# Norms of input plus branch over alpha, the input carried as its two rounded halves

## The chip, the cores and the metric

The kernel runs on one core of a Trainium2 chip. Its time is device microseconds of that core. It is written in the Bass language: every engine (TensorE for matmuls, VectorE, ScalarE, GpSimd, and SyncE for transfers) has its own program, and semaphores order them. The kernel's time is the median of several runs; times of single instructions come from one profiled execution.

## The reference

Two layers of a first block (FFN, mixer of attention and mLSTM, FFN) are followed by two layers of a second block. The change is in the second block alone:

```python
DN_ALPHA = (2 * DEPTH) ** 0.25          # DEPTH = 2
LN_EPS = 1e-5

def second_block(x, ...):
    cos, sin = rotary_tables(x.shape[1])
    for l in range(DEPTH):
        y = hybrid_mixer(x, ..., cos, sin)             # ends in concat(ya, yb, yc, yd) @ w_o
        x = layer_norm(DN_ALPHA * x + y, ln1_g[l], ln1_b[l])
        y = conv_gated_ffn(x, ...)                     # ends in (silu(gate) * val) @ w_down
        x = layer_norm(DN_ALPHA * x + y, ln2_g[l], ln2_b[l])
    return x

def layer_norm(x, g, b):
    mu = mean(x);  var = mean((x - mu) ** 2)
    return (x - mu) * rsqrt(var + LN_EPS) * g + b
```

x has 256 tokens of 1024 features in fp32; the FFN width is 2816. A layer norm does not change when its input is divided by alpha, if its eps is divided by alpha squared.

## The kernel before

All weights come as units of 128x1024 fp32 through a ring: SyncE loads `w_raw`, ScalarE rounds it to `w_hi` (line 542), VectorE forms the remainder `w_lo` (line 1033), TensorE waits for both (`split_done`). Activations are kept as a rounded half and a remainder too (`h_hi`, `h_lo`; `ya_hi`, `ya_lo`; `act_hi`, `act_lo`), and every product is three matmuls on rounded operands: hi x hi, lo x hi, hi x lo (lines 1732 to 1734 with the weight tile loaded into the array and the activation streamed; lines 1738 to 1740 with the activation loaded and 512 columns of weights streamed). The order is written out by hand: each engine's program calls its steps unit by unit, and a step waits on a semaphore that another engine counts up.

In the second block, the residual x lives in `x_residual` with features on partitions, and `h_hi`, `h_lo` hold its rounded half and its remainder. The norms are taken with tokens on partitions: the last product of a stage (`w_o`, or `w_down`) adds up in the two accumulators `acc_tok`, 128 tokens x 1024 features each. The residual is brought into the same accumulator by TensorE, as a matmul with a scaled identity: `carry(t, k)` adds 128 features of token half t (line 2134). There are 16 carries per stage:

- `mixer2`: eight for t = 0 in a row behind unit 19 (`VALUES_AT`), eight for t = 1 in a row at the start of the second half of `tail_norm`.
- `conv_ffn`: one for t = 0 behind each of the first eight down units, eight for t = 1 in `tail_norm`.

`tail_norm` runs the last four units of a stage for t = 0, then the carries and the same four units for t = 1; meanwhile VectorE and ScalarE take the statistics of t = 0 and norm it (`layer_norm`, `y_tok`), TensorE turns the result back (`turn_norm`, line 2129), and it is rounded for the next stage.

The branch reaches the accumulator through these roundings, each a pair of ScalarE (hi) and VectorE (lo): `c_round` / `c_rest` (spatial gating), `d_round` / `d_rest` (pooling, with a per-feature scale), `o_round` / `o_rest` (attention, twice per mixer, unit 21), and in the FFN `act32`, the product of gate and value (line 1479), which `act_round` / `act_rest` split.

## Time and profile before

| what | value |
|---|---|
| median of 3 runs | 2004.33 us (2003.71 to 2005.48) |
| profiled execution | 2003.57 us, its span 2001.7 us |
| TensorE busy | 1983.4 us, 99% |
| TensorE weight loads | 1735.8 us, 87% |
| VectorE busy | 1265.5 us, 63% |
| ScalarE busy | 1100.1 us, 55% |
| mean granted TensorE clock | 0.998 |

The page names each group of instructions by its line, its engine, output<-inputs and shape. A tile name without number stands for all its buffers: `acc` is `acc_tok`, `stream` the four banks, `act` is `act32`. An fp32 matmul leaves two records and two weight loads, a matmul on rounded operands (fp32r) one of each. Matmul records overlap, so the time that one takes is read from the distance of starts or from the chain of waits, not from its duration.

### The profile page before, as it was taken

The page shows a single profiled execution, that of the slowest core. Times are in us where ns is not written, and L with a number is a line of the kernel's source. Part 1 is how long each engine was busy: PE and PEld are TensorE (multiplying, and loading weights), DVE is VectorE, ACT ScalarE, POOL GpSimd, SP SyncE. Part 2 cuts the span into 40 slices and gives each one's busy share as a digit, 9 for nine tenths or more (in the row PEclk, how much of TensorE's full clock was granted, in tenths as well). Part 3 has the DMA queues.
Part 4 walks back from the last instruction along what each step waited for, and adds up shares of the span by engine and source line. Part 5 has one row for each costly group of instructions (what it writes and reads, how often), then busy time and mean ns, then how long its engine had stood idle before and what let it go on. Part 6 is the DMA issues. An engine that isn't in the chain of part 4 may idle for free.

```text
span 2001.7 us, 29971 instructions
## 1 busy us (share of the span) xinstructions
PE 1983.4 (99%) x11884; PEld 1735.8 (87%) x11884; DVE 1265.5 (63%) x2121; ACT 1100.1 (55%) x1709; POOL 6.5 (0%) x17
## 2 busy tenths in 40 slices
PE   9999999999999999999999999999999999999998
PEld 7888898998888888889989988888899997889997
DVE  5555787566555655567846665557567776657775
ACT  5445676465544644466664564447455556545554
POOL 0000000000000000000000000000000000000000
PEclk9999999999999999999999999999999999999999
DMA  8665545555666466655464556664336665335662
GB/s 281 188 187 174 166 130 168 162 155 158 209 188 189 148 199 190 189 149 168 134 192 131 164 190 196 187 186 144 116 115 181 184 186 164 116 106 169 183 186 84
DMA packets 93690, 335.86 MB, mean 168 GB/s; under 512 B 10224, under 2 KB 12528, under 8 KB 93552
## 3 DMA queue, kind: packets, MB, share of 16 engines
q1 hardware_dynamic: 92112, 328.51, 53.7%
q0 software_dynamic: 720, 4.37, 0.5%
q8 instruction: 95, 1.56, 0.3%
q10 hardware_dynamic: 720, 1.07, 0.2%
q14 instruction: 43, 0.35, 0.1%
HBM read 332.86 MB, written 1.05 MB: 167 GB/s over the span
## 4 chain that ended last, share of the span: by engine, by line
PE 95%; DVE 3%; ACT 1%; issue 1%; DVEq 0%; ACTq 0%
PE stream L1732 11%; PE stream L1733 11%; PE stream L1734 10%; PE stream L1738 9%; PE stream L1740 9%; PE stream L1739 9%; PE acc L1738 8%; PE acc L1740 8%; PE acc L1739 8%; PE stream L1828 1%; PE acc L2279 1%; DVE w_lo L1033 1%; PE acc L2134 1%; PE stream L1791 1%; PE stream L1758 0%
## 5 line engine op out<-in xcount | busy, mean ns | idle before, releaser
L1033 DVE TENSOR_TENSOR w_lo<-w_raw,w_hi 128x1024 fp32r<-128x1024 f32 x624 | 760.8, 1223 | 407.9 <-ACT w_hi L542 407.0
L542 ACT ACTIVATE w_hi<-w_raw 128x1024 fp32r<-128x1024 f32 x624 | 655.5, 1055 | 420.1 <-PE stream L1740 207.9
L1732 PE MATMUL stream<-h_hi,w_hi 128*128 128x256 f32 (+1 forms) x1504 | 434.2, 289 | 2.5 <-DVE h_lo L1433 2.5
L1734 PE MATMUL stream<-h_hi,w_lo 128*128 128x256 f32 (+1 forms) x1504 | 424.7, 282 | 0.0
L1733 PE MATMUL stream<-h_lo,w_hi 128*128 128x256 f32 (+1 forms) x1504 | 424.6, 282 | 0.0
L1738 PE MATMUL stream<-w_hi,h_hi 128*128 128x512 f32 x864 | 342.1, 396 | 2.2 <-DVE h_lo L1433 2.2
L1740 PE MATMUL stream<-w_lo,h_hi 128*128 128x512 f32 x864 | 337.3, 390 | 0.0
L1739 PE MATMUL stream<-w_hi,h_lo 128*128 128x512 f32 x864 | 336.8, 390 | 0.0
L1732 PEld LDWEIGHTS stream<-h_hi,w_hi 128*128 128x128 f32 x1504 | 287.8, 191 | 10.5 <-issue 7.1
L1733 PEld LDWEIGHTS stream<-h_lo,w_hi 128*128 128x128 f32 x1504 | 288.0, 191 | 0.8
L1734 PEld LDWEIGHTS stream<-h_hi,w_lo 128*128 128x128 f32 x1504 | 287.6, 191 | 0.0
L1738 PE MATMUL acc<-w_hi,act_hi 128*128 128x512 f32 x528 | 211.2, 400 | 1.4 <-DVE act_lo L1105 1.3
L1740 PE MATMUL acc<-w_lo,act_hi 128*128 128x512 f32 x528 | 206.3, 391 | 0.0
L1739 PE MATMUL acc<-w_hi,act_lo 128*128 128x512 f32 x528 | 206.3, 391 | 0.0
L1738 PEld LDWEIGHTS stream<-w_hi,h_hi 128*128 128x128 f32 x864 | 162.5, 188 | 35.8 <-issue 2.5
L1740 PEld LDWEIGHTS stream<-w_lo,h_hi 128*128 128x128 f32 x864 | 162.4, 188 | 34.4
L1739 PEld LDWEIGHTS stream<-w_hi,h_lo 128*128 128x128 f32 x864 | 162.7, 188 | 31.8
L1467 DVE SCALAR_TENSOR_TENSOR conv_tiles<-stream,params,conv_tiles 128x255 f32<-128x255 f32 (+1 forms) x168 | 81.0, 482 | 66.0 <-ACT conv_tiles L870 63.0
L1738 PEld LDWEIGHTS acc<-w_hi,act_hi 128*128 128x128 f32 x528 | 99.4, 188 | 22.5 <-DVE w_lo L1033 3.0
L1740 PEld LDWEIGHTS acc<-w_lo,act_hi 128*128 128x128 f32 x528 | 99.1, 188 | 21.7
L1739 PEld LDWEIGHTS acc<-w_hi,act_lo 128*128 128x128 f32 x528 | 99.5, 188 | 17.8
L870 ACT ACTIVATE conv_tiles<-stream,params 128x256 f32<-128x256 f32 x84 | 47.5, 565 | 117.7 <-PE stream L1734 117.7
(308 smaller groups left out, 2291.4 us busy)
## 6 DMA issues: line engine op xcount, KB each, us to landing
w_raw<-in_w_up SPq DMA_DIRECT2D x264, 512.0 KB, 3.7
w_raw<-in_w_mix SPq DMA_DIRECT2D x228, 512.0 KB, 3.7
w_raw<-in_w_down SPq DMA_DIRECT2D x132, 512.0 KB, 3.7
params<-in_params POOLq DMA_DIRECT2D x4, 859.5 KB, 5.5
out_x<-x_residual SPq DMA_DIRECT2D x4, 256.0 KB, 2.4
constants<-in_consts POOLq DMA_DIRECT2D x1, 832.0 KB, 8.1
x_residual<-in_x ACTq DMA_DIRECT2D x3, 256.0 KB, 7.4
x_residual<-in_x SPq DMA_DIRECT2D x1, 256.0 KB, 3.5
```

What stands on the lines that cost most here:

```text
L542: nc.scalar.activation(w_hi[:, u % RING], w_raw[:, u % RAW], ACT.Copy).then_inc(hi_ready, 1)
L870: nc.scalar.activation(cbuf[:, 2 * (i % 2) + side_i], conv_tile(i, side_i), ACT.Identity, scale=p2("conv_w", (2 * 2 + side_i) * NF + i), b ...
L1033: nc.vector.tensor_tensor(w_lo[:, u % RING], w_raw[:, u % RAW], w_hi[:, u % RING].bitcast(F32), ALU.subtract).then_inc(split_done, 1)
L1467: r = nc.vector.scalar_tensor_tensor(out=cbuf[:, s, back:], in0=conv_tile(i, side_i)[:, 0:T - back], scalar=p2("conv_w", ((2 - back) * 2 + ...
L1732: nc.tensor.matmul(dst, w_hi[:, s, w], hi, start=first, stop=False)
L1733: nc.tensor.matmul(dst, w_hi[:, s, w], lo, start=False, stop=False)
L1734: return nc.tensor.matmul(dst, w_lo[:, s, w], hi, start=False, stop=last)
L1738: nc.tensor.matmul(dst, hi, w_hi[:, s, w], start=first, stop=False)
L1739: nc.tensor.matmul(dst, lo, w_hi[:, s, w], start=False, stop=False)
L1740: return nc.tensor.matmul(dst, hi, w_lo[:, s, w], start=False, stop=last)
L1791: r = nc.tensor.matmul(turned[1][:, t:t + 1], h32[:, k, half(t)], ones_model[:, 0:1], start=(k == 0), stop=(k == KT - 1))
L1828: r = nc.tensor.transpose(turned[c % 2][:, half(2 * i + t)], cbuf[:, 2 * (c % 2) + t, half(i)], ident)
```

## The change

The norms are taken of x + branch/alpha. The carry has no factor any more, so its operands can be the two halves that exist already, `h_hi` and `h_lo`, with the rounded identity `ident_rounded` of the first block's mixer. The factor 1/alpha moves into the roundings of the branch: into `c_round`, `o_round` (a scale), `c_rest`, `o_rest` and `act32` (scalar_tensor_tensor for tensor_tensor), and for the pooling into a small tile `pool_scale`, made once per layer. The norm's eps becomes `eps3`. The tile `ident_alpha` and TensorE's wait for it go.

```diff
@@ build
+        eps3, _ = sb("eps3", [P, 1])
-        ident_alpha, _ = sb("ident_alpha", [P, P])
+        pool_scale, _ = sb("pool_scale", [P, 2])
@@ ScalarE: layer_norm, mixer2, start
-                                         bias=eps2[:]).then_inc(act_step, 1)
+                                         bias=eps3[:]).then_inc(act_step, 1)
...
                 def c_round():
                     act.wait_ge(c_turned, l + 1)
-                    nc.scalar.activation(ya_hi[:, 4:6].rearrange("p a t -> p (a t)"), side[3][:],
-                                         ACT.Copy).then_inc(cd_hi, 1)
+                    nc.scalar.activation(ya_hi[:, 4:6].rearrange("p a t -> p (a t)"), side[3][:], ACT.Copy,
+                                         scale=1.0 / ALPHA).then_inc(cd_hi, 1)
                 def d_round():
                     act.wait_ge(d_mixed, l + 1)
+                    act.wait_ge(alpha_ready, l + 1)
                     for ct in range(2):
                         r = nc.scalar.activation(ya_hi[:, 6 + ct], bank[2][:, ct * T:(ct + 1) * T], ACT.Copy,
-                                                 scale=p2("pool_scale", ct))
+                                                 scale=pool_scale[:, ct:ct + 1])
...
-                                         ACT.Copy).then_inc(o2_hi, 1)
+                                         ACT.Copy, scale=1.0 / ALPHA).then_inc(o2_hi, 1)
...
-            act.wait_ge(init, 4)
+            act.wait_ge(init, 5)
@@ VectorE: conv_ffn, mixer2, start
-                    nc.vector.tensor_tensor(act32[:, i % 2], silu_g[:, i % 2], cbuf[:, 2 * (i % 2) + 1],
-                                            ALU.mult).then_inc(gated, 1)
+                    nc.vector.scalar_tensor_tensor(out=act32[:, i % 2], in0=silu_g[:, i % 2], scalar=1.0 / ALPHA,
+                                                   in1=cbuf[:, 2 * (i % 2) + 1], op0=ALU.mult,
+                                                   op1=ALU.mult).then_inc(gated, 1)
...
                 def o_rest(t):
                     dve.wait_ge(o2_hi, l * 2 + t + 1)
-                    nc.vector.tensor_tensor(ya_lo[:, 0:4, half(t)], bank[2 * t + 1][:].rearrange("p (k q) -> p k q", k=4),
-                                            ya_hi[:, 0:4, half(t)].bitcast(F32), ALU.subtract).then_inc(ab_split, 1)
-
-                if l == 0:
-                    nc.vector.tensor_scalar(ident_alpha[:], ident, ALPHA, None, ALU.mult).then_inc(alpha_ready, 1)
+                    nc.vector.scalar_tensor_tensor(out=ya_lo[:, 0:4, half(t)],
+                                                   in0=bank[2 * t + 1][:].rearrange("p (k q) -> p k q", k=4),
+                                                   scalar=1.0 / ALPHA, in1=ya_hi[:, 0:4, half(t)].bitcast(F32),
+                                                   op0=ALU.mult, op1=ALU.subtract).then_inc(ab_split, 1)
+
+                nc.vector.tensor_scalar(pool_scale[:], p2("pool_scale", 0, 2), 1.0 / ALPHA, None,
+                                        ALU.mult).then_inc(alpha_ready, 1)
...
+            nc.vector.memset(eps3[:], LN_EPS / ALPHA ** 2).then_inc(init, 1)
@@ TensorE: carry, mixer2
             def carry(t, k):
-                nc.tensor.matmul(acc_tok[t][:, k * P:(k + 1) * P], xr[:, k, half(t)], ident_alpha[:], start=False,
-                                 stop=False)
+                for x in (h_hi, h_lo):
+                    nc.tensor.matmul(acc_tok[t][:, k * P:(k + 1) * P], x[:, k, half(t)], ident_r[:], start=False,
+                                     stop=False)
...
-                        if i == V_OUT:
-                            pe.wait_ge(alpha_ready, 1)
```

`c_rest` changes as `o_rest` does, and `d_rest` reads `pool_scale` as `d_round` does.

The order of TensorE's instructions, at the first down unit of the first convolution FFN (`act_hi`, `act_lo` are the gated tile's halves), before:

```order
L1740 MATMUL acc<-w_lo,act_hi 128x512
L2134 MATMUL acc<-ident_alpha,x_residual 128x128
L1732 MATMUL stream<-h_hi,w_hi 128x256 [waits conv2_done,split_done]
L1733 MATMUL stream<-h_lo,w_hi 128x256
L1734 MATMUL stream<-h_hi,w_lo 128x256
```

and now:

```order
L1747 MATMUL acc<-w_lo,act_hi 128x512
L2142 MATMUL acc<-ident_rounded,h_hi 128x128
L2142 MATMUL acc<-ident_rounded,h_lo 128x128
L1739 MATMUL stream<-h_hi,w_hi 128x256 [waits conv2_done,split_done]
L1740 MATMUL stream<-h_lo,w_hi 128x256
L1741 MATMUL stream<-h_hi,w_lo 128x256
```

One fp32 instruction, which the trace shows as two passes, becomes two instructions on rounded operands; what stands around it keeps its place.

VectorE's order in the first mixer, from the attention's row scales to the tail's first statistics, before:

```order
L1609 RECIPROCAL row_scales<-row_sums 128x16 [waits e2_ready]
L1613 TENSOR_TENSOR o_tok<-stream,row_scales 128x512 [waits o2_ready,dve_step]
L1613 TENSOR_TENSOR o_tok<-stream,row_scales 128x512 [waits o2_ready]
L1033 TENSOR_TENSOR w_lo<-w_raw,w_hi 128x1024 [waits hi_ready] x2
L1620 TENSOR_TENSOR ya_lo<-stream,ya_hi 128x4x128 [waits o2_hi] x2
L1033 TENSOR_TENSOR w_lo<-w_raw,w_hi 128x1024 [waits hi_ready]
L1404 BN_STATS ln_stats<-acc 128x6 [waits acc_left]
```

and now:

```order
L1613 RECIPROCAL row_scales<-row_sums 128x16 [waits e2_ready]
L1617 TENSOR_TENSOR o_tok<-stream,row_scales 128x512 [waits o2_ready,dve_step]
L1617 TENSOR_TENSOR o_tok<-stream,row_scales 128x512 [waits o2_ready]
L1035 TENSOR_TENSOR w_lo<-w_raw,w_hi 128x1024 [waits hi_ready] x2
L1624 SCALAR_TENSOR_TENSOR ya_lo<-stream,ya_hi 128x4x128 [waits o2_hi] x2
L1035 TENSOR_TENSOR w_lo<-w_raw,w_hi 128x1024 [waits hi_ready]
L1406 BN_STATS ln_stats<-acc 128x6 [waits acc_left]
```

`o_rest` stands where it stood, in the other form; nothing else here moved.

## Rows read from the trace of the kernel before

**Rows 1.** Page: span, part 1, part 4 (chain that ended last) by engine.

```profile
span 2001.7 us, 29971 instructions
...
PE 1983.4 (99%) x11884; PEld 1735.8 (87%) x11884; DVE 1265.5 (63%) x2121; ACT 1100.1 (55%) x1709; POOL 6.5 (0%) x17
...
PE 95%; DVE 3%; ACT 1%; issue 1%; DVEq 0%; ACTq 0%
```

**Rows 2.** Waits of TensorE, two of seven: us in total, times, longest.

```profile
PE stream L2129 <- ACT y_tok L828: 3.9, 2, 3.3
...
PE acc L1738 <- DVE ya_lo L1620: 0.3, 2, 0.2
```

**Rows 3.** First convolution FFN: us, PE, PEld, DVE, ACT, POOL busy, clock, DMA.

```profile
1480.00:1672.00 192.00, 192.00 (x1384) 181.64 (x1384) 138.83 (x209) 107.49 (x161) 0.60 (x1) 1.00 0.60 180
```

**Rows 4.** Line 2134, the carries: count, ns min/median/max, first and last start.

```profile
L2134 PEld LDWEIGHTS acc<-ident_alpha,x_residual x128: 187/192/192, 1449.0 to 1985.7; 128*128 128x128 f32 x128
L2134 PE MATMUL acc<-ident_alpha,x_residual x128: 270/275/275, 1449.2 to 1985.8; 128*128 128x128 f32 x128
```

**Rows 5.** The chain that ended last, two of its pieces: start us, us, what.

```profile
1441.27 1.73 PE stream L2299 x16
...
1449.40 1.78 PE acc L2134 x16
```

**Rows 6.** TensorE's timeline behind a group of eight: start us, us, engine, line, what.

```profile
1450.94 0.48 PE L1738 MATMUL acc<-w_hi,ya_hi 128*128 128x512 f32 x1
1451.25 0.40 PE L1739 MATMUL acc<-w_hi,ya_lo 128*128 128x512 f32 x1
1451.49 0.39 PE L1740 MATMUL acc<-w_lo,ya_hi 128*128 128x512 f32 x1
```

**Rows 7.** TensorE's timeline, a lone carry in the convolution FFN.

```profile
1532.59 0.38 PE L2134 MATMUL acc<-ident_alpha,x_residual 128*128 128x128 f32 x2
...
1532.93 0.28 PE L1733 MATMUL stream<-h_lo,w_hi 128*128 128x256 f32 x1
1533.05 0.28 PE L1734 MATMUL stream<-h_hi,w_lo 128*128 128x256 f32 x1
```

**Rows 8.** TensorE's timeline, narrow rounded products, first and last of 46, and their exit.

```profile
1473.03 0.27 PE L1734 MATMUL stream<-h_hi,w_lo 128*128 128x128 f32 x1
...
1478.06 0.28 PE L1734 MATMUL stream<-h_hi,w_lo 128*128 128x128 f32 x1
...
1495.10 0.33 PE L1732 MATMUL stream<-h_hi,w_hi 128*128 128x256 f32 x1
1495.27 0.28 PE L1733 MATMUL stream<-h_lo,w_hi 128*128 128x256 f32 x1
```

**Rows 9.** VectorE's groups by shape: count | busy us, mean ns | idle.

```profile
L1479 DVE TENSOR_TENSOR act<-silu_g,conv_tiles 128x256 f32<-128x256 f32 x44 | 18.7, 425 | 1.5
...
L1221 DVE SCALAR_TENSOR_TENSOR attn_scores<-attn_scores,attn_coeffs 128x256 f32<-128x256 f32 x16 | 7.7, 480 | 0.0
...
L1251 DVE SCALAR_TENSOR_TENSOR ya_lo<-stream,attn_norm_scaled,ya_hi 128x512 fp32r<-128x512 f32 x8 | 6.0, 750 | 7.5 <-ACT ya_hi L694 7.5
...
L1620 DVE TENSOR_TENSOR ya_lo<-stream,ya_hi 128x512 fp32r<-128x512 f32 x4 | 2.6, 682 | 0.0
```

**Rows 10.** Chain before TensorE's wait for `ya_lo`, then two timeline rows.

```profile
1772.38 1.23 DVE w_lo L1033
1773.61 1.21 DVE ya_lo L1620 x2
...
1772.26 1.07 ACT L932 ACTIVATE ya_hi<-stream 128x512 fp32r<-128x512 f32 x2
...
1774.95 0.47 PE L1738 MATMUL acc<-w_hi,ya_hi 128*128 128x512 f32 x1 [0.15 <-DVE ya_lo L1620]
```

**Rows 11.** Timeline, VectorE and ScalarE: start, and second mixer's first unit.

```profile
4.79 0.91 ACT L993 ACTIVATE h_hi<-x_residual,gains 128x256 fp32r<-128x256 f32 x2
...
1688.51 4.86 DVE L1033 TENSOR_TENSOR w_lo<-w_raw,w_hi 128x1024 fp32r<-128x1024 f32 x4 [1.75 <-ACT w_hi L542]
```

More of the change, by code:

```diff
@@ L1544, in c_rest @@
                     dve.wait_ge(cd_hi, l * 2 + 1)
-                    nc.vector.tensor_tensor(ya_lo[:, 4:6].rearrange("p a t -> p (a t)"), side[3][:],
-                                            ya_hi[:, 4:6].rearrange("p a t -> p (a t)").bitcast(F32),
-                                            ALU.subtract).then_inc(cd_split, 1)
+                    nc.vector.scalar_tensor_tensor(out=ya_lo[:, 4:6].rearrange("p a t -> p (a t)"), in0=side[3][:],
+                                                   scalar=1.0 / ALPHA,
+                                                   in1=ya_hi[:, 4:6].rearrange("p a t -> p (a t)").bitcast(F32),
+                                                   op0=ALU.mult, op1=ALU.subtract).then_inc(cd_split, 1)
                 def rotate(pair):
@@ L1602, in d_rest @@
                         r = nc.vector.scalar_tensor_tensor(out=ya_lo[:, 6 + ct], in0=bank[2][:, ct * T:(ct + 1) * T],
-                                                           scalar=p2("pool_scale", ct), in1=ya_hi[:, 6 + ct].bitcast(F32),
+                                                           scalar=pool_scale[:, ct:ct + 1], in1=ya_hi[:, 6 + ct].bitcast(F32),
                                                            op0=ALU.mult, op1=ALU.subtract)
```

## The prediction

> **What bounds the kernel now.** I read the page's head and its chain first. TensorE is busy 99% of the span and holds 95% of the chain that ended last; VectorE holds 3% and ScalarE 1% [rows 1]. So a microsecond counts if it is TensorE's own issue time, or if another engine keeps TensorE waiting. The list of TensorE's waits comes second: for the second block it names waits for the normed rows (`y_tok`, 3.9 us, and `h_lo`), which the change leaves as they are, and 0.3 us for `ya_lo`, which it touches [rows 2]. `act_lo` of the convolution FFN (line 1455) is not in the list. By stretches, TensorE is busy for all of the 192.00 us of the first convolution FFN [rows 3]. The change touches TensorE's carries, and on VectorE one operation in each kind of rounding. So there are two questions: what a carry costs TensorE in issue time, and whether a longer VectorE operation lies in front of a TensorE wait.
>
> **What the change removes on TensorE.** A carry before is one fp32 matmul of `x_residual` with `ident_alpha`. The trace has 128 matmul records and 128 weight loads for it, so each of the 64 carries (2 layers x 2 stages x 16) is two passes [rows 4]. They come in six groups of eight (one in each mixer, one in each of the four tails) and 16 that stand alone, one behind each of the first eight down units of a convolution FFN. A group of eight, 16 records, takes 1.78 us of the chain, 0.111 us a pass [rows 5]. A lone carry: from its start at 1532.59 to the second product behind it at 1532.93 are 0.34 us, less one 256-column slot of 0.12: 0.22 [rows 7].
>
> **What it adds there.** Two products with rounded operands, `h_hi` and then `h_lo` against `ident_rounded`, 128x128 each: 128 matmuls, again 128 weight loads. The kernel before has products of just this form, rounded and 128 columns wide, in the first units of a convolution FFN, each with its own weight load (there the weight tile is loaded and `h_hi` or `h_lo` streams; here `h_hi` or `h_lo` is loaded and the identity streams). From the start at 1473.03 to that at 1478.06 there are 45 steps, 5.03 / 45 = 0.1118 us each [rows 8]. A group of eight then costs 16 x 0.1118 = 1.79 us where it cost 1.78, and a lone pair 2 x 0.1118 = 0.22 where it cost 0.22. Sum over six groups and 16 pairs: 6 x 0.01 + 16 x 0.00 = +0.1 us.
>
> Why halving the work inside the array would not show: the columns do not set the step. Fp32 matmuls with 64 columns, those of `values`, stream half as much per weight load as the carries, and 16 of their records still take 1.73 us, 0.108 each [rows 5]. What all of these have in common is a weight load of 128 columns per record. The weight loads stay 128 in number, so this term cannot fall below 16 x 0.108 = 1.73 for a group, that is 64 x 2 x (0.108 - 0.111) = -0.4 us in all. For the upper end: leaving a run of narrow rounded products has cost a bubble, the first 256-column product behind it taking 0.17 us (1495.27 - 1495.10) where 0.12 is usual [rows 7, 8]. The 1.78 and the 0.22 of the old carries hold their own exit (1451.25 - 1450.94 = 0.31 where 0.24 follows, [rows 6]). Charged in full to the new ones at 22 exits it would be 22 x 0.05 = +1.1 us. I take +0.1, since in both forms the weight loads behind the exit are one step of 0.11 apart and the bubble only shows the stream catching up with them; the bounds are -0.4 and +1.1.
>
> The Trainium skill speaks against this reading: "FP8 and Floating Point Precision", section "TensorE Precision Notes", has true fp32 as four passes through the array. Two of them would go, and with 53 ns for 128 columns at 2.4 GHz the estimate is 64 x 2 x 53 ns, 6.8 us less. The same skill's "TensorE: Matmul & The Clock Gate", section "LDWEIGHTS", sets a weight load by its columns, P / 1.2, an estimate of 107 ns for 128 columns whatever streams; by that rule nothing is gained, and the 64-column rows, at 0.108 us, agree with it.
>
> **VectorE.** Four kinds of TENSOR_TENSOR become SCALAR_TENSOR_TENSOR.
> - `o_rest`, `ya_lo` from PSUM, 128x512, four times (two in a row in each mixer): 682 ns now; the same operation in the new form stands in the first block's mixer at 751 ns, so +69 ns each [rows 9]. This pair ends a chain with no slack: VectorE `w_lo` 1.23, `ya_lo` x2 1.21, and then TensorE, which sat idle 0.15 us for it, in both layers alike (the second is shown) [rows 10]. TensorE's next units, and behind them the tail, wait for this. So 2 x 0.069 = 0.14 us a layer, **+0.28 us** in all. The wait is open already, so nothing covers it; 0 would need the two operations to be no longer in the new form, which the 751 excludes.
> - `act` of the convolution FFN, 128x256 from SBUF, 44 times: 425 ns now, 480 ns for a SCALAR_TENSOR_TENSOR of that size from SBUF [rows 9], so 44 x 0.055 = 2.4 us of VectorE. Behind it on VectorE wait `w_lo` and the next conv pair; ScalarE's rounding waits for it. It is hidden by VectorE's idle time, 192 - 139 = 53 us in the stretch (22 of the 44 stand there, 1.2 us), while TensorE has none [rows 3], and by the distance of four steps between a gated tile and the down product that reads it. 0; if that cover were gone, +2.4.
> - `c_rest`, twice, grows by the same 0.07 us, but the product that reads it (unit 18 of the mixer) comes six units later, and the `d_rest` had the new form before: 0. With that cover gone it would be +0.14.
> - `pool_scale`, 128x2, replaces the larger `ident_alpha` once and is new in the second layer, there before the `w_lo` that began at 1688.51 after 1.75 us of idle time [rows 11], far more than any VectorE operation of this list takes: 0. ScalarE's new wait for it, in `d_round`, comes some fifteen units later, with the `v_tok` evictions queued behind it and TensorE's `values` waiting for them: 0, since the value is there long before. `eps3` is one memset more at the start, before ScalarE's first activation at 4.79 [rows 11], which waits for it, its function table and the input: 0.
>
> ScalarE's copies of `c_round` and `o_round` now carry a constant scale. No row separates that price. The two `o_round` run from 1772.26 to 1773.33, and the second `ya_lo`, which needs the second of them, starts after 1774.1 (1773.61 and half of 1.21) [rows 10]: up to 0.8 us of growth is covered, 0.
>
> **Sum.** +0.1 + 0.28 = +0.4 us on the profiled execution: 2003.57 (span 2001.7 and 1.9 around it) becomes 2004.0. That execution lies 0.8 us below the median of 2004.33; put on the median, **2004.7 us**. What can be told from no change here is about 0.2%, 4 us.
>
> **Rivals.**
> 1. *The streaming sets the carry's time, not the weight load.* The pair would cost 2 x 0.056 and not 0.22: 64 x 0.11 = 7.1 us less, from 2004.7: 1997.6 us, faster. For it: each pass of the fp32 carry holds the array for 0.111 us, and 128 columns at the full clock of 2.4 GHz would need half of that, so streaming twice per pass would explain the step as well. Against it: 128-column rounded products at 0.1118 and 64-column fp32 ones at 0.108 [rows 5, 8]. Chance 5%. The skill's four-pass rule is the general form of this rival.
> 2. *The pair loads its weights in the open.* A loaded `h_hi` is used for only 128 columns and then replaced. If the load of `h_lo` did not hide behind so short a product, a step would take about what a 512-column product takes, 0.23: 128 x (0.23 - 0.111) = +15.2 us, 2019.9 us, slower. It decides once a step is over 0.142 us (128 x 0.031 = 4 us). The narrow products speak against it: each of them loads 128 columns of weights for 128 streamed ones, at 0.1118 [rows 8]. Chance 3%.
> 3. *VectorE falls behind in the convolution FFN.* For it: gate, rounding and remainder of `act` pass from VectorE to ScalarE and back, and each hand-over would be later. If each of the 44 delays reached TensorE: +2.4 + 0.4 = 2007.1 us, still no measurable change. Against it: no idle time of TensorE in that stretch [rows 3]. Chance 4%.
> 4. The forecast, including the exits at full price (2005.8): 88%.
>
> **How the numbers follow.** The forecast's own bounds are -0.4 + 0.28 and +1.1 + 0.28, so 2004.2 to 2005.7, and the runs of before themselves spread from 2003.71 to 2005.48. With both, and rival 3, 2001.8 to 2007.8 leaves out rivals 1 and 2 and little else. Faster 0.06, same 0.89, slower 0.05: rival 1 with one point of scatter between runs, then the forecast with rival 3 less three points of scatter, then rival 2 with two.
>
> **What would show it.** In the profile after: 128 matmul records on the carry's line (64 with `h_hi`, 64 with `h_lo`) in place of the 128 of the fp32 carry; groups of eight at 1.79 us in the chain, lone pairs at 0.22; `ya_lo` of the second block at 751 ns with TensorE's idle before the product behind it up from 0.15 to 0.29 us; `act` at 480 ns, `act_lo` of line 1455 still in no wait of TensorE. A group at 0.9 us would be rival 1, one above 2.3 us rival 2, a wait for `act_lo` or `conv_tiles` in the convolution FFN rival 3. The forecast is wrong if the step of the carries leaves 0.108 to 0.12 us.

## The result: 7 us slower, and none of it in the changed instructions

| | before | changed |
|---|---|---|
| median of 20 executions each, side by side | 2004.61 us | 2012.39 us |
| lowest of them | 2003.45 us | 2009.74 us |
| ratio, 95% interval | | 1.0057 (1.0036 to 1.0079) |
| profiled execution, its span | 2003.57, 2001.7 us | 2010.84, 2008.9 us |
| mean granted clock there | 0.998 | 0.998 |

The changed kernel is slower by 0.4 to 0.8%; the forecast was 2004.7 us, in a range of 2001.8 to 2007.8. To read the numbers below, one thing is needed: every kernel here has executions in which TensorE's clock stood at half for some stretch, which lengthens them by about 5 or about 20 us. Where that matters the lowest time of a kernel stands beside its median; the two profiled executions above have the same clock, and differ by 7.2 us of span.

The page of the changed kernel, head and part 4, answers to [rows 1]:

```profile
span 2008.9 us, 29972 instructions
PE 1989.8 (99%) x11884; PEld 1734.5 (86%) x11884; DVE 1265.2 (63%) x2123; ACT 1100.4 (55%) x1709; POOL 6.4 (0%) x17
PE 96%; DVE 2%; ACT 1%; issue 1%; DVEq 0%; ACTq 0%
```

TensorE has as many records as before (11884) and is busy 6.4 us longer; its weight loads are 1.3 us shorter. VectorE and ScalarE did not change. So the time is TensorE's own. The waits of TensorE confirm it (us in total, times, longest), beside [rows 2]:

```profile
PE stream L2136 <- ACT y_tok L829: 5.1, 2, 3.3
PE stream L1739 <- DVE h_lo L1435: 2.5, 2, 1.2
PE stream L1745 <- DVE h_lo L1435: 2.0, 1, 2.0
PE stream L1835 <- DVE conv_tiles L1100: 1.9, 4, 0.5
PE stream L2389 <- DVE ln_half L1668: 1.5, 1, 1.5
PE acc L1745 <- DVE act_lo L1107: 1.0, 4, 0.3
```

The wait for `y_tok` grew by 1.2 us, 1.0 of it at one place. TensorE stood at half clock for 3.4 us in both traces, ahead of this wait before (from 1678.5 us) and behind it now (from 1687.6 us); before and then changed:

```profile
1681.94 1.09 PE L2129 MATMUL stream<-constants,y_tok 128*128 128x128 f32 x8 [0.64 <-ACT y_tok L828]
```

```profile
1686.73 1.23 PE L2136 MATMUL stream<-constants,y_tok 128*128 128x128 f32 x8 [1.87 <-ACT y_tok L829]
```

The wait for `ya_lo` is no longer listed: two starts that stood 0.53 us apart at it now stand 0.48 apart, as the products ahead of it take longer. What was changed on TensorE is read from the line of the carries (ns shortest, median, longest; first and last start), beside [rows 4], and from the chain (start us, us), beside [rows 5]:

```profile
L2142 PE MATMUL acc<-ident_rounded,h_hi x64: 222/274/277, 1452.5 to 1992.9; 128*128 128x128 f32 x64
L2142 PE MATMUL acc<-ident_rounded,h_lo x64: 272/275/277, 1452.5 to 1993.0; 128*128 128x128 f32 x64
```

```profile
1444.50 1.73 PE stream L2307 x16
1452.65 1.73 PE acc L2142 x16
1466.84 1.73 PE acc L2142 x16
1671.63 1.73 PE acc L2142 x16
```

128 records, and each group of eight at 1.73 us in the chain, 0.108 a record, where the fp32 carries had 1.78 (e4 below shows that the exit takes this back). But look at the start: the first group starts at 1452.65, and before it started at 1449.40 [rows 5]. **3.25 us are lost before the first changed instruction of TensorE has run**, nearly all of it in the first block (3.15 at 1383 us), whose code is the same. If the same instruction is looked up in both traces all along the program, the changed kernel is behind by 0.1 us at 506, 2.5 at 887, 3.15 at 1383, 4.75 at 1673, 6.2 at 1800 and 7.1 at 1971: it creeps in through the down products of the FFNs, in both blocks, and some of it goes again in the mixers of the first block (0.7 us at 400, 0.1 at 506). One step of 1.6 us, between 1673 and 1685, is the wait for `y_tok` and the stretch at half clock beside it.

The groups by shape say which instructions these are (count | busy us, mean ns). First three groups of before:

```profile
L1739 PE MATMUL acc<-w_hi,act_lo 128*128 128x512 f32 x528 | 206.3, 391 | 0.0
L1733 PE MATMUL stream<-ya_lo,w_hi 128*128 128x256 f32 x128 | 36.2, 283 | 0.0
L1739 PE MATMUL stream<-w_hi,h_lo 128*128 128x512 f32 x864 | 336.8, 390 | 0.0
```

and the same three of the changed kernel:

```profile
L1746 PE MATMUL acc<-w_hi,act_lo 128*128 128x512 f32 x528 | 208.8, 395 | 0.0
L1740 PE MATMUL stream<-ya_lo,w_hi 128*128 128x256 f32 x128 | 35.7, 279 | 0.0
L1746 PE MATMUL stream<-w_hi,h_lo 128*128 128x512 f32 x864 | 337.1, 390 | 0.0
```

The name gives the streamed tile first and the loaded one second. With `act_lo` loaded a product takes 4 to 5 ns more, with `ya_lo` streamed 4 ns less, with `h_lo` loaded as much as before. In the timeline the down product shows it as a distance of starts. First and last of twelve in a row, before and then changed:

```profile
1529.84 0.40 PE L1738 MATMUL acc<-w_hi,act_hi 128*128 128x512 f32 x1
...
1532.36 0.39 PE L1740 MATMUL acc<-w_lo,act_hi 128*128 128x512 f32 x1
```

```profile
1533.52 0.40 PE L1745 MATMUL acc<-w_hi,act_hi 128*128 128x512 f32 x1
...
1536.09 0.40 PE L1747 MATMUL acc<-w_lo,act_hi 128*128 128x512 f32 x1
```

2.52 / 11 = 0.2291 us a step before, 2.57 / 11 = 0.2336 now. If all distances from one start to the next of TensorE's records are summed by what the first of the two streams and has loaded, nearly the whole difference is accounted for:

| streamed, loaded | records | before us | changed us | difference |
|---|---|---|---|---|
| `w`, `act` | 1584 | 374.6 | 381.8 | +7.2 |
| `w`, `ya` | 192 | 48.3 | 48.9 | +0.6 |
| `ya` or `ym`, `w` | 768 | 92.5 | 91.1 | -1.4 |
| `w`, `h` | 3072 | 711.2 | 712.3 | +1.1 |
| `h`, `w` | 4704 | 573.1 | 572.5 | -0.6 |
| all others, the carries among them | 1563 | 195.9 | 195.9 | 0.0 |

### The profile page after: what moved, and what is told of

It is laid out like the page before. It is cut to its first block, busy times and chain, and to the rows that moved or that the text cites. A ratio compares the mean times of both kernels' runs of the same rounds, so it can differ in the third digit from the quotient of the medians.

```text
span 2008.9 us, 29972 instructions
## 1 busy us (share of the span) xinstructions
PE 1989.8 (99%) x11884; PEld 1734.5 (86%) x11884; DVE 1265.2 (63%) x2123; ACT 1100.4 (55%) x1709; POOL 6.4 (0%) x17
## 4 chain that ended last, share of the span: by engine, by line
PE 96%; DVE 2%; ACT 1%; issue 1%; DVEq 0%; ACTq 0%
PE stream L1739 11%; PE stream L1740 10%; PE stream L1741 10%; PE stream L1745 9%; PE stream L1747 9%; PE stream L1746 9%; PE acc L1745 8%; PE acc L1747 8%; PE acc L1746 8%; PE stream L1835 1%; PE acc L2287 1%; PE acc L2142 1%; PE stream L1798 1%; DVE w_lo L1035 1%; DVE x_residual L1065 0%
## 5 line engine op out<-in xcount | busy, mean ns | idle before, releaser
L871 ACT ACTIVATE conv_tiles<-stream,params 128x256 f32<-128x256 f32 x84 | 47.4, 565 | 117.6 <-PE stream L1741 117.6
```

Of the source, the lines that this page charges most:

```text
L871: nc.scalar.activation(cbuf[:, 2 * (i % 2) + side_i], conv_tile(i, side_i), ACT.Identity, scale=p2("conv_w", (2 * 2 + side_i) * NF + i), b ...
```

## The experiments

Two theories at first: the placement of the tiles, against something that the new instructions do (through the carries, or through VectorE). Each run stood beside runs of the kernel before on the same chip; their medians were 2004.34, 2004.63, 2004.03 and 2004.28 us for the four sets (e1 to e4, e5 to e8, e9 to e12, e13 to e15), their lowest 2003.45, 2003.35, 2003.22 and 2003.21; each set had a chip of its own. "Steps" are mean distances from a product's start to the next start, in ns, without the stretches at half clock and without pauses; names are streamed, loaded. `w` with `h_hi` is `w_hi`, and `h_lo`, `w` includes the 128-column products.

**e1: the tile alone.** The kernel before with the new tile in its place, unused.

```diff
+        eps3, _ = sb("eps3", [P, 1])     # behind eps2, never read
```

> The kernel before with one unused 64-byte tile behind eps2, so that every tile behind it, act_hi, act_lo, ya_hi and ya_lo among them, moves by 64 bytes as in the changed kernel; no instruction changes. Place theory: the step of products that load act_hi or act_lo as weights goes from about 228.5 to 233 ns as in the changed kernel, 1460 steps x 4.5 ns = 6.5 us, so +6 to +7 us over before (2010 to 2011). Carry theory (the new instructions cost it): no change, 2004 to 2005. Clock: if the moved tiles also cause the executions at 2029 and 2049 us, some appear here; if the carries cause them, none.

Measured: lowest 2010.29 us, median 2029.74, ratio 1.0065 (1.0028 to 1.0102). The lowest is 0.6 us above the changed kernel's 2009.74; the median is high because seven of the twelve executions had a long stretch at half clock (below). Steps of `w`, `act_lo` 233.3 ns (changed 233.2, before 228.5), of `ya_lo`, `w` 117.6 (117.4, 119.9). A tile of 64 bytes that nothing reads gives the whole loss.

**e2: the whole change, with the tile declared last.**

```diff
-        eps3, _ = sb("eps3", [P, 1])     # behind eps2
...
+        eps3, _ = sb("eps3", [P, 1])     # behind the last tile
```

> The changed kernel with eps3 placed behind all other tiles, so that act_hi, act_lo, ya_hi and ya_lo lie where they lay before. Place theory: 2004 to 2005.5 us, the act steps back at 228.5 ns, and the terms of my prediction (+0.1 for carries, +0.28 for o_rest) are what is left. Carry theory: stays at 2010 to 2012. Clock: if executions at 2029 us and above appear here too, it isn't the places that cause them.

Measured: 2003.91 us, ratio 0.9982 (0.9960 to 1.0004). All of the change is in it, and none of the loss. Its chain, waits and VectorE groups give the change's own price:

```profile
1449.73 1.74 PE acc L2142 x16
```

```profile
PE acc L1745 <- DVE ya_lo L1624: 0.3, 2, 0.2
```

```profile
L1481 DVE SCALAR_TENSOR_TENSOR act<-silu_g,conv_tiles 128x256 f32<-128x256 f32 x44 | 18.7, 425 | 1.5
L1624 DVE SCALAR_TENSOR_TENSOR ya_lo<-stream,ya_hi 128x512 fp32r<-128x512 f32 x4 | 2.6, 682 | 0.0
L1548 DVE SCALAR_TENSOR_TENSOR ya_lo<-acc,ya_hi 128x512 fp32r<-128x512 f32 x2 | 1.4, 692 | 0.8 <-ACT ya_hi L921 0.8
```

The three operations in the new form last 425, 682 and 692 ns, as in the old form (425, 682 and 692). What has a scalar per partition lasts longer in the same trace:

```profile
L1253 DVE SCALAR_TENSOR_TENSOR ya_lo<-stream,attn_norm_scaled,ya_hi 128x512 fp32r<-128x512 f32 x8 | 6.0, 749 | 7.6 <-ACT ya_hi L695 7.6
L1223 DVE SCALAR_TENSOR_TENSOR attn_scores<-attn_scores,attn_coeffs 128x256 f32<-128x256 f32 x16 | 7.7, 478 | 0.0
```

The wait for `ya_lo` is 0.3 us as it was [rows 2].

**e3: the carry alone**, in the kernel before. It leaves the factor alpha of the residual out.

```diff
-                nc.tensor.matmul(acc_tok[t][:, k * P:(k + 1) * P], xr[:, k, half(t)], ident_alpha[:], start=False,
-                                 stop=False)
+                for x in (h_hi, h_lo):
+                    nc.tensor.matmul(acc_tok[t][:, k * P:(k + 1) * P], x[:, k, half(t)], ident_r[:], start=False,
+                                     stop=False)
```

> The kernel before with the new carry alone (h_hi and h_lo with the rounded identity); the factor alpha of the carry is left out, and all else including the places is as before. Place theory: +0.1 us (between -0.4 and +1.1) over before. Carry theory: +6 to +8 us. Clock: the rounded pair fills the array less than the fp32 passes did, right before the tail's waits; if that lets the granted clock fall, executions 19 us and more above the fastest appear here as often as in the changed kernel (10 of 20).

Measured: 2004.81 us, ratio 0.9990 (0.9967 to 1.0012), groups of eight at 1.73 to 1.74 us. One of its twelve executions took 2462.95 us, at a mean granted clock of 0.742; nothing like it came again, and its cause is not known.

**e4: the change in its old places, with the carry kept in fp32** (by the unscaled identity).

```diff
-                for x in (h_hi, h_lo):
-                    nc.tensor.matmul(acc_tok[t][:, k * P:(k + 1) * P], x[:, k, half(t)], ident_r[:], start=False,
-                                     stop=False)
+                nc.tensor.matmul(acc_tok[t][:, k * P:(k + 1) * P], xr[:, k, half(t)], ident, start=False,
+                                 stop=False)
```

> The changed kernel with the old places and the carry as one fp32 matmul with the unscaled identity: what is left of the change are the scalar_tensor_tensor forms, the scales, pool_scale and eps3. Place theory and my prediction: +0.28 us over before. If the VectorE forms cost more than that, it shows here: above +1 us would refute hidden act operations. Clock: executions at 2029 us only if VectorE's forms cause them.

Measured: 2005.61 us, ratio 1.0006 (0.9978 to 1.0035), groups at 1.78. So in the chain a rounded group is 0.05 us shorter in the same place. The exit takes it back. From the last product ahead of a group to the third behind it the kernel before takes 1451.49 [rows 6] - 1449.01 = 2.48 us, and e2 1451.82 - 1449.35 = 2.47; before and then e2:

```profile
1449.01 0.39 PE L1740 MATMUL acc<-w_lo,ya_hi 128*128 128x512 f32 x1
```

```profile
1449.35 0.39 PE L1747 MATMUL acc<-w_lo,ya_hi 128*128 128x512 f32 x1
...
1451.31 0.45 PE L1745 MATMUL acc<-w_hi,ya_hi 128*128 128x512 f32 x1
1451.59 0.40 PE L1746 MATMUL acc<-w_hi,ya_lo 128*128 128x512 f32 x1
1451.82 0.39 PE L1747 MATMUL acc<-w_lo,ya_hi 128*128 128x512 f32 x1
```

To the nanosecond it is 2.475 or 2.476 us for each of the six groups in the kernel before, in e2, in e3 and in e4, and 0.685 us around each of the 16 lone carries. The new carry costs what the old one did. What remains is the placement, and the next runs ask what it is that counts in it.

**e5 to e8: which tile, and how far.** e5 makes the idle tile of e1 128 bytes. e6 moves `act_hi` and `act_lo` alone by 64 in the kernel before. e7 moves them by 64 more in the changed kernel. e8 moves `h` by 64 and what follows by 128 in the kernel before.

```diff
+        eps3, _ = sb("eps3", [P, 32])    # e5
...
+        place[0] += 64                   # e6, e7: ahead of act_hi; e8: ahead of h_hi, again behind h_lo
```

> The kernel before with an unused tile of 128 bytes behind eps2: everything behind it moves by 128 bytes, not by 64. If what counts is where a tile lies within 128 bytes: 2004 us, act step 228.5 ns, and executions above 2025 us no more often than before. If every move away from the old place costs: 2010 us as with 64 bytes.

> The kernel before with act_hi and act_lo alone moved by 64 bytes. If the loss is theirs alone, as the steps of the changed kernel say (1460 steps x 4.5 ns): fastest executions +6.0 to +6.5 us, ya products unchanged at 227.5 / 240 ns. Clock: if the long stretch at the lower clock behind the first mixer of the second block comes from these products too, executions near 2029 us and above appear as with everything moved (7 of 12); if it comes from another tile, they don't.

> The changed kernel with act_hi and act_lo moved 64 bytes further, so that these two lie at a multiple of 128 bytes as before, while ya, ym and the rest stay moved by 64. If the act products alone cost: fastest executions at 2003.5 us less the gain of the products that stream ya and ym (768 steps x 2.4 ns = 1.8 us in the first block) plus the loss of those that load ya (0.7 us), so 2002 to 2003 us, faster than both kernels by some 1 us. If the carry or another tile costs: 2009 to 2011.

> The kernel before with h_hi and h_lo moved by 64 bytes (what lies behind them moves by 128). They are loaded as weights in 3072 matmuls with 512 columns and streamed in 4512 with 256. If loading from a moved tile costs 4.7 ns and streaming from one gains 2.4 ns, as act and ya showed: +14.4 - 10.8 = +3.6 us; the step of stream<-h_hi,w_hi goes from 119.5 to 117.5 ns and that of stream<-w_hi,h_hi from 228 to 232. If the effect is not general but act's own: no change.

| run | lowest, median us | ratio | `w`,`act_lo` | `w`,`h_lo` | `h_lo`,`w` | `ya_lo`,`w` |
|---|---|---|---|---|---|---|
| before (steps of its first trace) | 2003.35, 2004.63 | | 228.5 | 227.0 | 119.0 | 119.9 |
| e5 | 2010.37, 2032.62 | 1.0074 (1.0034 to 1.0114) | 232.5 | 227.9 | 119.3 | 118.6 |
| e6 | 2015.44, 2030.71 | 1.0091 (1.0056 to 1.0126) | 233.3 | 227.2 | 119.2 | 119.9 |
| e7 | 2010.12, 2029.00 | 1.0078 (1.0043 to 1.0113) | 232.3 | 227.4 | 119.4 | 117.4 |
| e8 | 2017.47, 2036.64 | 1.0112 (1.0064 to 1.0161) | 232.4 | 233.3 | 116.9 | 118.5 |

e6 is the sharpest: only `act` moved, and only its products grew, by 4.8 ns, while those with `ya` stayed at 119.9. Its lowest time is worse than e1's because it lacks the gain on `ya` and `ym` and its best execution has a short fall of the clock (0.996 on the mean). e8 brings the loss to `h` as well: 6.3 ns on products that e1 to e7 left within 1 ns, and 2.1 ns of gain where `h` is streamed. That 128 bytes cost nearly what 64 do is what e5 and e7 add. It refutes two of the expectations: the raster of 128 bytes, by which e5 would have given 2004 us and e7 2002 to 2003 (e7 landed on the number of its other branch, with the loss still on `act`), and e8's sum of +3.6 us, where the lowest time is 14 us up, since `act`, now at 128, pays too.

**e9 to e12: distance or address, and the side that gains.** e9 moves everything by 64, e11 what lies behind by 512. e10 moves the weights alone by 64, so that the loaded `w` stands 64 bytes above what is streamed. e12 is the changed kernel in its old places (e2), with `ya` and `ym` of the first block 64 bytes further, to keep that gain alone.

```diff
+        place[0] += 64                   # e9: ahead of the first tile
...
+        place[0] += 64                   # e10
         w_hi, _ = sb("w_hi", [P, RING, KT * P], F32R)
         w_lo, _ = sb("w_lo", [P, RING, KT * P], F32R)
+        place[0] += 448
...
+        eps3, _ = sb("eps3", [P, 128])   # e11: the idle tile at 512 bytes
```

> The kernel before with every tile, the weight ring included, moved by 64 bytes. Relative theory (the step of a matmul depends on how the address of its loaded tile lies to that of its streamed one): nothing changes, 2004 us, steps 228.5 and 227.4 ns. Absolute theory (each tile has to lie at its own multiple): act and h products at 233 ns, 256-column products at 117.5 ns, fastest execution some +10 us.

> The kernel before with w_hi and w_lo moved by 64 bytes and all that lies behind them by 512. Relative theory: every product that pairs the ring with an activation tile changes, act, h and ya with 512 columns to 233 ns (4848 steps x 5 ns = +24 us), all 256-column products to 117.5 ns (5280 steps x -2.4 = -13 us), so +11 us in the fastest executions. If only the place of the loaded activation counts: 512-column steps stay at 227 to 229.

> The kernel before with an unused tile of 512 bytes behind eps2. The loaded pieces are 512 bytes long, so if the distance counts within 512 bytes, 2004 us and act steps at 228.5 ns or, if the remaining 1 ns against the h products comes from the distance within 1024, 227.5 ns and -1.5 us. If any move costs: 2010 us.

> The changed kernel with eps3 behind all tiles and, in the first block's mixer alone, ya and ym moved by 64 bytes, where they are only streamed; mixer2 has its own ya at the old place. Relative theory: act, h and mixer2's ya as before (228.5, 227.4), ya and ym streamed at 117.5 to 118 where they took 120 ns: 768 x -2.3 = -1.8 us, so 2002 us in the fastest executions and the clock as in the kernel before. If the low clock comes with any moved tile: executions above 2020 us in half of the runs.

| run | lowest, median us | ratio | `w`,`act_lo` | `w`,`h_hi` | `h_lo`,`w` | `ya_lo`,`w` |
|---|---|---|---|---|---|---|
| before (steps of its first trace) | 2003.22, 2004.03 | | 228.5 | 227.4 | 119.0 | 119.9 |
| e9 | 2003.49, 2007.27 | 1.0011 (0.9985 to 1.0036) | 228.5 | 227.3 | 118.9 | 119.9 |
| e10 | 1990.14, 1990.89 | 0.9948 (0.9920 to 0.9975) | 228.5 | 230.5 | 114.9 | 113.8 |
| e11 | 2003.51, 2004.95 | 0.9993 (0.9971 to 1.0015) | 228.4 | 227.3 | 118.9 | 119.9 |
| e12 | 2002.76, 2015.60 | 1.0033 (1.0003 to 1.0063) | 228.4 | 227.4 | 119.3 | 117.4 |

Moving everything changes nothing, and moving by 512 changes nothing: what counts is the distance between the loaded and the streamed tile, within 512 bytes at most. And the side matters: with the loaded tile 64 bytes above the streamed one, products of 512 columns with an activation loaded lose 5 ns (e1), while products of 256 columns with a weight loaded gain 4 to 6 (e10). **e10 beats both kernels by this alone**: 13.1 us between the lowest times, with no instruction changed. Its expectation had the sign wrong, +11 us: it gave every distance of 64 bytes the same price on either side. Nor is the gain free. By the steps, e10's products with a weight loaded save 25 us, those with an activation loaded lose 9 (with `h_hi` 3 ns each, with `h_lo` nothing), and some 2.4 us of new waits for VectorE open up as TensorE gets faster. In the groups, one of before and then three of e10:

```profile
L1733 PE MATMUL stream<-h_lo,w_hi 128*128 128x256 f32 x1440 | 407.0, 283 | 0.0
```

```profile
L1735 PE MATMUL stream<-h_lo,w_hi 128*128 128x256 f32 x1440 | 400.1, 278 | 0.0
L1735 PE MATMUL stream<-ya_lo,w_hi 128*128 128x256 f32 x128 | 35.4, 276 | 0.0
L1741 PE MATMUL stream<-w_hi,h_lo 128*128 128x512 f32 x864 | 336.8, 390 | 0.0
```

283 became 278 for `h_lo`, and 276 for `ya_lo`. e12 kept its gain of 2.5 ns on `ya_lo`, `w`, which on all products that stream `ya` or `ym` was 1.4 us in the table of the result; its lowest time is 0.5 us below that of the kernel before, no more than scatter. Its median is worse, for six of its twelve executions had the long fall of the clock (below).

**e13 to e15: the change in the better places, and the curve.** e13 is e2 with e10's edit. e14 and e15 are e10 with 128 and 256 in place of 64.

```diff
+        place[0] += 128                  # e14, ahead of w_hi, and 384 behind w_lo; e15: 256 and 256
```

> The changed kernel with its small tile last (every other tile where the kernel before has it), and the weight tiles w_hi and w_lo 64 bytes further on, all behind them 512. Theory: the change itself costs nothing and the distances set the rest, so it gives what moving the weight tiles gave without the change: 1990 to 1992 us (1990.9 there), steps of h_lo on w_hi near 115 ns and of w_hi on act_lo near 228.5. Rival: the change costs something that only shows when TensorE is faster elsewhere (VectorE's longer operations become the bound): 1993 us or more, with a new wait for act_lo or ya_lo.

> The kernel before with w_hi and w_lo 128 bytes further on and all behind them 512, so that the loaded w stands 128 bytes above the streamed activations. Theory (the step depends on the distance): with everything behind at +128 instead, w streamed and the activation loaded above it took 232.5 ns and w loaded below took 118.6; here, with w above, narrow products of 116 to 119 ns and wide ones near 228.5 to 231, so 1992 to 2001 us. Rival: only a distance of 64 bytes gains, and 128 gives the time of before, 2003.5 to 2005.5 us.

> As the run before, but w_hi and w_lo 256 bytes further on: half way round the 512 bytes, so above and below are the same. Theory (steps depend on the distance within 512 bytes): narrow products between 117 and 120 ns, wide ones 227 to 232, time 1998 to 2012 us. Rival: only the nearest 64 or 128 bytes matter, and the steps are those of before (119.0 and 228.5), 2003.5 to 2005.5 us.

| run | lowest, median us | ratio | `w`,`act_lo` | `w`,`h_hi` | `h_lo`,`w` | `ya_lo`,`w` |
|---|---|---|---|---|---|---|
| e13 | 1988.38, 1995.79 | 0.9963 (0.9927 to 0.9999) | 228.3 | 231.1 | 114.6 | 114.8 |
| e14 | 2019.04, 2029.48 | 1.0113 (1.0067 to 1.0159) | 231.6 | 232.5 | 118.0 | 118.7 |
| e15 | 2003.53, 2007.65 | 1.0014 (0.9989 to 1.0039) | 228.4 | 227.4 | 118.9 | 119.9 |

e13: the changed kernel reaches 1988.4 us where e10 reached 1990.1, so the change costs nothing in these places too. The two ran on different chips, so the 1.8 us between them are not shown to be a gain. Its median, 1995.79, lies above the expected 1990 to 1992, since five of its twelve executions against three of e10's had the long fall; the new wait that the rival asked for did not come. Both expectations for e14 failed: 128 bytes are no smaller gain but a loss, 16 us, with 232 to 233 ns on every wide product. And e15 behaves as no distance at all, as the rival said. Together with e5 (128 on the other side: 232.5 and 118.6, e14 231.6 and 118.7) the steps repeat after 256 bytes: 0 and 256 alike, 128 alike from both sides, and 64 above unlike 64 below. Between multiples of 64 bytes, and for other pairs of widths, nothing was tried. Why the distance counts is open. The trace shows that the load for the next product starts with the product before it (the load of `act_lo` at 1529.85 us beside the product at 1529.84 in the kernel before), so the streamed tile may meet the tile that is being loaded for the next product and not its own; both lie at the same place in every kernel here, and no run separates them.

```profile
1529.85 0.19 PEld L1739 LDWEIGHTS acc<-w_hi,act_lo 128*128 128x128 f32 x1
```

**What stays open: the falls of the clock.** In e1's profiled execution, by windows (us; TensorE, its loads, VectorE, ScalarE, GpSimd busy with counts; clock; DMA), and then the kernel before in one of the same windows:

```profile
1470.00:1480.00 10.00, 8.77 (x54) 7.53 (x53) 6.62 (x12) 4.75 (x9) 0.00 (x0) 0.95 0.27 66
1480.00:1490.00 10.00, 10.00 (x50) 10.00 (x49) 4.82 (x9) 6.46 (x12) 0.00 (x0) 0.50 0.29 94
1490.00:1500.00 10.00, 10.00 (x49) 10.00 (x48) 1.23 (x1) 1.06 (x2) 0.00 (x0) 0.50 0.19 52
1500.00:1510.00 10.00, 10.00 (x48) 10.00 (x48) 4.42 (x7) 3.74 (x6) 0.00 (x0) 0.50 0.17 54
1510.00:1520.00 10.00, 10.00 (x48) 10.00 (x49) 4.76 (x9) 3.74 (x6) 0.00 (x0) 0.51 0.34 105
1520.00:1530.00 10.00, 10.00 (x86) 10.00 (x85) 7.91 (x13) 5.27 (x8) 0.00 (x0) 1.00 0.45 152
```

```profile
1490.00:1500.00 10.00, 10.00 (x89) 10.00 (x88) 8.89 (x17) 7.44 (x12) 0.00 (x0) 1.00 0.60 166
```

A granted clock of 0.50 is the lower level, 1.2 GHz. It begins right where TensorE had idled behind the tail of a mixer (8.77 us busy of 10) and holds for 41 us, in which TensorE issues 48 to 50 records per 10 us for 75 to 92 before: some 20 us lost. In the traces of e5, e6 and e7 a fall of 10.2 us stands at this place and the one of 41 us behind the second mixer's tail, near 1804 us. Of 142 executions of the kernel before 10 were over 15 us above the lowest; of the changed kernel 8 of 20 (e3's expectation counts 10); of e1 7, e5 9, e6 7 (9 by the granted clock, since its lowest is disturbed too), e7 8, e12 6, e13 5 and e10 3 of 12, e8 4 and e14 3 of 6. In e2, e3, e4, e9, e11 and e15, which share the steps of before, it was 7 of 72, the one of 2462.95 us among them. So placements with other steps see it more often, most clearly those that lose, and e12; 3 of 12 for e10 and 5 of 12 for e13, which gain, are few to tell from the 2 of 12 of e4, e9 and e15. But TensorE's pause ahead of it, 1.63 to 1.65 us from one start to the next, is there in all of them, and what makes the clock fall in one execution and not in the next was not found. It adds to the medians and is no part of the 7 us, which the lowest executions show.

## Why the prediction was wrong, point by point

- **The term that failed is the 0 of `eps3`.** The text said that it is "one memset more at the start" and priced its instruction, not its place; with that the sum took the other 11,756 records of TensorE as unchanged. Its place cost +7.2 us on `act`, +0.6 on `ya` loaded, -1.4 on `ya` and `ym` streamed. That is +6.4 us. e1 shows it alone, e2 the change without it.
- **Carries, +0.1 us (-0.4 to +1.1): right within the bounds.** It measured 0.0. A group takes 1.73 in the chain, not 1.79, and the exit gives the 0.05 back (2.476 us over all in both forms). 128 loads and 128 records, as stated. That the weight load sets this step was argued from fp32 passes at 0.108, and e2 to e4 agree with it; but the number of loads stayed the same in every run, so it is not shown. The exits' bubble (+1.1) did not come on top.
- **`o_rest`, +0.28 us: mis-sized.** It measured 0. The row taken for the price (751 ns in the text, 750 in [rows 9]) has a scalar per partition; here the scalar is a constant, and the new form takes the old one's 682 ns. The text said that 751 "excludes" 0. It didn't.
- **`act`, 2.4 us hidden: mis-sized and harmless**, for the same reason: 425 ns in both forms, not 480.
- **`c_rest`, `pool_scale`, the new wait, ScalarE's scale: 0, right**, by e2's waits.
- **Rival 1** (streaming sets the carry's time, 1997.6 us): false, 1.73 and not 0.9 a group. The Trainium skill's "FP8 and Floating Point Precision", section "TensorE Precision Notes", has four passes for fp32, from which the prediction's estimate was 6.8 us less. No run here shows that: e3, which changes nothing else, stands at 0.999 (0.9967 to 1.0012) of before, and 6.8 us would be 0.9966, just outside; the 2.476 us of a group in both forms say the same. The Trainium skill's "TensorE: Matmul & The Clock Gate", section "LDWEIGHTS", has P / 1.2, an estimate of 107 ns for 128 columns; the traces agree with it, with 0.108 us a record in rounded form and 0.111 in fp32.
- **Rival 2** (loads in the open): false, the groups' records are 0.108 apart. **Rival 3** (VectorE behind): false, the only wait for `act_lo` lies in the first block, 1.3 us before and in e2, 1.0 in the changed kernel.
- The sign "the forecast is wrong if the step of the carries leaves 0.108 to 0.12 us" was not enough: the step stayed, and the time left. It looked only at what had been thought of.

The chance for slower, 0.05, had one mechanism in it. No row of the trace of before could give the price, but the diff showed that a tile was put in the middle of an allocation in which the operands share a raster, and a chance for that was due.

## What to carry to other kernels

A declaration is part of a change: compare the addresses of all tiles before and after, not only the instructions, and put new small tiles last until the effect of their place has been looked at. When the time moves and the touched rows don't, line up the same instruction in both traces along the whole program; a loss that starts ahead of the change is not in its instructions. In a kernel bound by TensorE, try 64 bytes between the weights and the activations on purpose: here it was worth 13 us of 2004, for 512 bytes a partition. But look at both kinds of product: the same 64 bytes gained on one kind and lost on the other, and the side decides which.

## What the hardware did that I had not expected

- A product's step depends on the distance of address between the loaded and the streamed tile: 512 columns with an activation loaded 227 to 228.5 ns at 0, 233 at 64 above, 232 at 128, and with the activation 64 below 230.5 (`h_hi`) or as at 0 (`h_lo`); 256 columns with a weight loaded 119.9 (`ya_lo`) at 0, 113.8 with the weight 64 above, 117.4 with it 64 below, 118.7 at 128, 119.9 at 256. Only the distance counts (e9).
- A scalar_tensor_tensor with a constant scalar lasts as long as tensor_tensor (682 and 682 ns from PSUM at 512 columns, 425 and 425 at 256), one with a scalar per partition some 55 to 70 ns longer (749 and 478 in the changed kernel).
- 128-column products on rounded operands take 0.108 us each in a row when the activation is loaded and the identity streamed, against 0.1118 for the narrow products of [rows 8], and two of them cost TensorE as much as one fp32 matmul of that size (2.476 us over a group in both forms).
- Half the clock for 41 us behind a stretch in which TensorE had idled, in some executions and not in others, and more often in some placements; its trigger is open.
